# A denoising trunk on one core: one modulation vector moves from the first attention on TensorE into the first FFN on VectorE

## What is computed

```python
def adaln(cond, w, b):
    m = jax.nn.silu(cond) @ w + b                  # w_ada[li]: (1024, 9 * 1024)
    return [t[:, None, :] for t in jnp.split(m, N_MOD, axis=-1)]

def ffn_sublayer(x, shift, scale, gate, g_pre, g_post, w_in, w_out):
    h = modulate(rmsnorm(x, g_pre), shift, scale)  # x * (1 + scale) + shift
    a, b = jnp.split(h @ w_in, 2, axis=-1)
    h = (jax.nn.silu(a) * b) @ w_out
    return x + FFN_RES * gate * rmsnorm(h, g_post)

for li in range(DEPTH):
    mp = adaln(c_ctx[None, :], w_ada[li], b_ada[li])
    ms = adaln(c, w_ada[li], b_ada[li])
    yp = ffn_sublayer(yp, mp[0], mp[1], mp[2], ...)
    ...                                            # mixer with mp[3], mp[4], mp[5]
    yp = ffn_sublayer(yp, mp[6], mp[7], mp[8], ...)
```

## Time and profile before

| | |
|---|---|
| median of 3 runs | 3009.32 us (3008.97 to 3010.02) |
| the profiled execution | 3009.04 us, of it the span 3007.2 us |
| granted clock of TensorE, mean | 0.996 |
| busy: TensorE, VectorE, ScalarE, GpSimd | 2956.2, 2209.8, 1152.2, 561.6 us |
| sub-layer 0 (first FFN) | from about 36 to 314 us |
| sub-layer 1 (first attention) | from about 328 to 460 us |

### The profile page before, as it was taken

How to read it: one execution, slowest core, us unless ns; L and a number is a source line. 1 busy time by engine, 2 the same in 40 slices (tenths; PEclk the granted TensorE clock), 3 DMA queues, 4 the chain that set the end, 5 groups by cost and what they waited for, 6 DMA issues and landing times.

```text
span 3007.2 us, 46610 instructions
## 1 busy us (share of the span) xinstructions
PE 2956.2 (98%) x18194; PEld 2749.9 (91%) x18194; DVE 2209.8 (73%) x2897; ACT 1152.2 (38%) x1966; POOL 561.6 (19%) x586
## 2 busy tenths in 40 slices
PE   7999999999999999999999999999999999999999
PEld 6999889999999998999899999979999999889998
DVE  6888678887987657888888576768888888775444
ACT  4222664223322424222422365553224222664222
POOL 1111112112111112111211144631112111211001
PEclk9999999999999999999999999999999999999999
DMA  9667445665665445766566443337675766333443
GB/s 306 211 215 215 140 91 187 212 211 170 217 213 175 119 128 173 223 213 199 178 213 201 134 118 104 95 99 231 211 216 181 220 212 197 112 81 114 127 128 95
DMA packets 589696, 517.76 MB, mean 172 GB/s; under 512 B 66773, under 2 KB 523046, under 8 KB 587686
## 3 DMA queue, kind: packets, MB, share of 16 engines
q1 hardware_dynamic: 588918, 514.53, 56.6%
q10 hardware_dynamic: 560, 0.25, 0.0%
HBM read 510.37 MB, written 4.33 MB: 171 GB/s over the span
## 4 chain that ended last, share of the span: by engine, by line
PE 91%; issue 4%; DVE 2%; POOL 1%; ACT 1%; DMA 1%; SPq 0%; DVEq 0%; POOLq 0%; another core or an unknown queue 0%; ACTq 0%
PE bank L1698 19%; PE bank L1700 19%; PE bank L1699 19%; PE bank L1752 9%; PE bank L1751 9%; PE bank L1750 9%; PE bank L1725 1%; PE bank L619 1%; PE bank L1715 1%; PE bank L644 1%; DVE h_hi L2266 1%; DMA ada_first<-w_ada 1%; DVE h_lo L2276 0%; POOL hg_kr L1497 0%; PE bank L1783 0%
## 5 line engine op out<-in xcount | busy, mean ns | idle before, releaser
L1698 PE MATMUL bank<-h_hi,w_hi 128*128 128x384 f32 x3328 | 1120.6, 337 | 0.0
L1700 PE MATMUL bank<-h_hi,w_lo 128*128 128x384 f32 x3328 | 1114.6, 335 | 0.0
L1699 PE MATMUL bank<-h_lo,w_hi 128*128 128x384 f32 x3328 | 1113.8, 335 | 0.0
L1947 ACT ACTIVATE w_hi<-raw 128x1024 fp32r<-128x1024 f32 x646 | 681.1, 1064 | 1020.1 <-PE bank L1700 481.6
L2109 DVE TENSOR_TENSOR w_lo<-raw,w_hi 128x1024 fp32r<-128x1024 f32 x648 | 810.4, 1274 | 310.9 <-ACT w_hi L1947 305.7
L1698 PEld LDWEIGHTS bank<-h_hi,w_hi 128*128 128x128 f32 x3328 | 625.3, 188 | 10.9 <-ACT tmp L1966 1.6
L1699 PEld LDWEIGHTS bank<-h_lo,w_hi 128*128 128x128 f32 x3328 | 625.4, 188 | 6.1
L1700 PEld LDWEIGHTS bank<-h_hi,w_lo 128*128 128x128 f32 x3328 | 625.2, 188 | 0.0
L2136 DVE SCALAR_TENSOR_TENSOR fold<-ada_raw,cond,fold 128x1024 f32<-128x1024 f32 x462 | 616.4, 1390 | 0.1
L2455 POOL TENSOR_TENSOR h_lo<-tmp,h_hi 128x384 fp32r<-128x384 f32 x176 | 250.2, 1421 | 1762.9 <-DVE h_hi L2180 1762.9
L1752 PE MATMUL bank<-w_hi,h_lo 128*128 128x512 f32 x1056 | 414.0, 392 | 0.0
(11 more groups left out here) (204 smaller groups left out, 2420.1 us busy)
## 6 DMA issues: line engine op xcount, KB each, us to landing
raw<-w_ffn_in SPq DMA_DIRECT2D x352, 512.0 KB, 5.0
ada_raw<-w_ada SPq DMA_DIRECT2D x264, 512.0 KB, 4.2
raw<-w_ffn_out SPq DMA_DIRECT2D x176, 512.0 KB, 4.8
raw<-w_hgrn_in SPq DMA_DIRECT2D x40, 512.0 KB, 4.0
g_rows<-g_dram SPq DMA_DIRECT2D x12, 1024.0 KB, 6.7
raw<-w_attn_qkv SPq DMA_DIRECT2D x24, 512.0 KB, 5.5
raw<-w_conv_in SPq DMA_DIRECT2D x24, 512.0 KB, 4.9
ada_first<-w_ada SPq DMA_DIRECT2D x16, 512.0 KB, 11.0
```

The source lines that it names most:

```text
L1698: mm(out, wh, h_hi[:, k, :], start=(k == 0), stop=False)
L1699: mm(out, wh, h_lo[:, k, :], start=False, stop=False)
L1700: last = mm(out, wl, h_hi[:, k, :], start=False, stop=(k == DC - 1))
L1947: A(w_hi[:, b % RING, :], raw[:, b % RAW, :], ACT.Copy).then_inc(w_hi_made, 1)
```

## The change

Sub-layer 0 folds six units, 2 to 7, and sub-layer 1 makes none. The six begin at steps 0, 4, 8, 11, 15 and 18: the units that have three steps fold three, three and two slabs in them. In sub-layer 0 alone, slabs are loaded two blocks later in the sequence, sums are written three blocks later (and spread one block after that), and a unit is added four steps behind its reduction instead of two. Two units are then left over for the attention: one is added where the one was before, the second behind `normalize(1)`. TensorE no longer waits for `mods_made` ahead of the first scores of either attention.

```diff
-    units_of = {0: (2, 7), 1: (7, 8), 2: (8, 13), 3: (13, 17), 4: (17, 17), 5: (17, 22), 6: (22, 26), 7: (26, 26),
+    units_of = {0: (2, 8), 1: (8, 8), 2: (8, 13), 3: (13, 17), 4: (17, 17), 5: (17, 22), 6: (22, 26), 7: (26, 26),
                 8: (26, 31), 9: (31, 36), 10: (36, 36), 11: (36, 36)}
     units_end = [units_of[s][1] for s in range(12)]
-    FOLD_F = 4
+    UNIT_STARTS = {5: (0, 4, 8, 12, 16, 20), 6: (0, 4, 8, 11, 15, 18, 21)}
+
+    def unit_starts(s):
+
+        u0, u1 = units_of[s]
+        return UNIT_STARTS[max(u1 - u0, 5)]
 
     def sums_of(s):
 
         u0, u1 = units_of[s]
-        return {FOLD_F * (u - u0 + 1): u for u in range(u0, u1)}
+        return {unit_starts(s)[u - u0 + 1]: u for u in range(u0, u1)}
 
     def mods_of(s):
 
-        return {f + 2: u for f, u in sums_of(s).items()}
+        return {f + (4 if s == 0 else 2): u for f, u in sums_of(s).items()}
...
     def spreads_of(s):
 
-        return {at_a(f) + 11: u for f, u in sums_of(s).items()}
+        return {at_a(f) + (14 if s == 0 else 11): u for f, u in sums_of(s).items()}
 
     def slabs_at(s, f):
 
-        u0, u1 = units_of[s]
-        u = u0 + f // FOLD_F
-        return [(u, 2 * (f % FOLD_F) + n) for n in range(2)] if u < u1 else []
+        starts = unit_starts(s)
+        for i, u in enumerate(range(*units_of[s])):
+            length = starts[i + 1] - starts[i]
+            if starts[i] <= f < starts[i + 1]:
+                per = -(-DC // length)
+                first = per * (f - starts[i])
+                return [(u, k) for k in range(first, min(first + per, DC))]
+        return []
...
-        pe.wait_ge(mods_made, units_end[s])
+        if units:
+            pe.wait_ge(mods_made, units_end[s])
         scores(0)
...
         split(b0 + 9)
-        add_left_over()
+        add_left_over(0)
...
             normalize(2 * j + 1)
+            if j == 0:
+                add_left_over(1)
...
-                        slabs.setdefault(at_a(f) + 3 + n, []).append(slab)
+                        slabs.setdefault(at_a(f) + (5 if s == 0 else 3) + n, []).append(slab)
```

More of the change, by code:

```diff
@@ L2197, in mixer @@
                 elif ph.kind == "qkv":
-                    dve_attn(dve, s, split, ada_add, mod_add, lambda: [mod_fold(u) for u in left_over(s)])
+                    dve_attn(dve, s, split, ada_add, mod_add, lambda i: [mod_fold(u) for u in left_over(s)[i:i + 1]])
                 if ph.kind in ("hgrn", "qkv"):
```

## The result

The changed kernel takes 3018.61 us (median of 6 runs, 3017.65 to 3019.63), the kernel before in the same comparison 3009.47 (6 runs). The ratio is 1.0032, with a 95% interval from 1.0020 to 1.0045: slower by 9 us, where 4.0 were forecast and the range ended at +7.5. Taken again later on another occasion it was 1.0033 (1.0021 to 1.0044). So the sign was right and the size was not; the time lies outside the range.

What follows compares the result with a forecast made beforehand. TensorE, which never rests in the first FFN, was taken as the bound. Terms: 6.1 + 0.3 - 1.4 - 1.05 = +4.0 us on a median of 3009.32, giving 3013.3 us; range 3007.5 to 3016.8.

Steps and rivals of the forecast that it cites:

- The end of the FFN: Last steps of the first FFN: extra folds and a weight block held by the gains write make TensorE 6.1 us late.
- block 64: First FFN's 64th weight block, issued right behind the gains write: claimed to land 16.3 us after that write.
- block 61: First FFN's 61st weight block: TensorE claimed to begin it 4.2 us late, waiting for VectorE's multiplication of step 20.
- Rival 1: End of first FFN: the gains write holds no close follower; 2.1 us lost there, -0.4 in all, 3008.9; chance 0.20.
- seem to stand in line: Gains write in the first FFN: 2,048 single elements, with later blocks of SP's queue held until the write ends.
- The first attention: Removing unit 7's work there frees 4.27 us of TensorE; a late weight block leaves only 1.4 gained.
- A10: First attention's weight block behind the spread of unit 7: issued 1.7 us after unit 6's addition, landing 3.7 later.
- the boundary's 0.3: Between first FFN and attention: VectorE 0.65 us late at most, half of it idle time later, so 0.3 lost.
- from there a microsecond is a microsecond: First attention: each microsecond that A10 comes later was taken to cost just one microsecond.
- The second attention: TensorE's wait for the left-over unit before the first scores goes: 1.05 us gained.
- "Nothing" in the middle: Middle of the first FFN: unit 7's added folds and reductions are hidden behind TensorE and cost nothing.
- rival 2: First attention: A10 lands 7 us after issue, so 1.9 lost, not 1.4 gained; +7.3 us, 3016.6; chance 0.20.

Runs made afterwards that it cites:

- e13: On e4's kernel, the first FFN's gains transposed by TensorE and written as 16 rows of 128 numbers: 3009.01 us, ratio 0.9994.
- e9: On e4's kernel, the first FFN's gains written as 128 rows of 16 numbers, unpermuted and so wrong: 3007.76 us, ratio 0.9991.
- e3: The changed kernel with the first FFN's gains written three blocks sooner: 3016.29 us, ratio 1.0027.
- e12: The changed kernel again, nothing changed, with a second trace: 3020.04 us, ratio 1.0033.
- e2: The changed kernel with the two slabs of step 0 loaded behind blocks 3 and 4, as before: 3017.09 us, ratio 1.0031.
- e4: The changed kernel with the spread of unit 7's sums moved behind the loads of A10 and the block after it: 3009.15 us, ratio 1.0001.
- e5: The changed kernel with 14 unread matmuls on TensorE ahead of head 4's rotation in the first attention: 3017.19 us, ratio 1.0022.
- e6: On e4's kernel, the first FFN's gains written from ScalarE's DMA queue instead of SP's: 3014.65 us, ratio 1.0013.
- e1: The kernel before, unchanged, run and traced again: 3008.42 us, ratio 0.9999.
- e7: On e4's kernel, the six units begin at steps 0, 3, 6, 10, 14 and 17: 3009.86 us, ratio 1.0000.
- e11: The changed kernel with e7's unit starts and the gains written right behind block 63's load, ahead of waiting slabs: 3010.22 us, ratio 1.0000.

## Why the prediction was wrong

**The end of the FFN: right in its size, and in each term but one wait.** In the trace of after step 18 is 4.19 us late; with that added, the prediction said the write at 281.4 (281.48 measured), block 64 landed at 297.7 (297.5), TensorE late by 4.2 before block 61 (4.31), low parts ready at 310.6 (309.45 + 1.02 = 310.47). The tail is 6.14 to 6.46 us late in four traces (0.35 more by TensorE), 6.1 was forecast. The division held too: without the elements 2.1 was forecast, and 2.29 (e13) and 2.26 (e9) were measured; without the extra folds as well, 0.11 is left. What the forecast had wrong is what TensorE does between: of its two waits the second, some 2 us before the last chunk, came in e3, e9 and e13 (1.66 to 1.68) but not in after, e12, e2, e4, e5 and e6. In these six TensorE stands 3.7 to 4.9 us before block 61, and the clock falls to 0.5 for 3 to 7 us. In after this cost nothing, since the low parts came no sooner; that the size came out all the same is in part luck. Where the wait was longest (e5 and e6, 4.9 and 4.8) the tail is at +7.40 and +6.99. Rival 1 is out: the write holds a block 0.8 us behind it for 15.3 us.

The mechanism behind it was half right. I wrote that the blocks behind the write "seem to stand in line", and quoted the ring order. From another queue the write held the block just as long (15.7 us), so it is not the place in line. Nor are the elements themselves slow: 1,836 of them pass in a microsecond, and the packets of the loads behind take 2.3 us each instead of 0.15.

**The first attention: the load right, its price wrong.** A10 was issued 1.9 us after unit 6 was added (1.7 forecast) and landed in 3.9 (3.7). From the tail to the second heads the four traces gain 0.8 to 2.2 us (2.25, 2.15, 0.78 and 1.53; 1.1 was forecast, 1.4 less the boundary's 0.3). But a step of the prediction then failed: "from there a microsecond is a microsecond". TensorE's 3 us without work are followed by some 7 us at the granted clock of 0.5, and 1.96 to 2.59 us more are lost by the third heads, in all four traces with that rest and in none of the thirteen without it. So from the tail to the third heads these traces do not gain the 1.1 us of the forecast but lose 0.1 to 1.2: after and e12 0.1 to 0.3, e2 and e3 1.1 to 1.2. The latter two have one more stretch at 0.5, near 326 us, as before's trace has near 320 and e1's has not. This is the largest mis-sized term that the runs could name. The longest rests in the rows ahead of the prediction were 1.05 and 1.32 us, and I looked at none of 3 us, though before's trace has one of 2.87 with the low clock behind it, at 1966 us: I bounded how late the load could be and not what a rest brings behind it.

**The second attention: right.** 1.13 to 1.15 against 1.05.

**"Nothing" in the middle: right.** TensorE comes to step 18 on time, VectorE 0.35 us late. The start is not the change's: e1 has the slow one as well.

**What stays open.** Put together, the steps give 6.3 - 1.7 + 2.3 - 1.1 = 5.8 us (the means of the four traces); those traces, set to step 18, end at +5.92 to +7.87; the medians of their three kernels say 8.4 to 10.3. A part of this gap is the trace that all are measured against: set against e1's, the same kernel, the four end at +8.8 to +10.7. Between 2.6 and 4.5 us of the medians have no place. In e4 there is no such gap (its steps give +0.5, its median is 1.3 over before's), but in e6, without the late load, there is (+0.2 and 5.4). The clock is large enough for it. On e12's chip its six runs have a mean granted clock of 0.9940, the 28 of before 0.9958; 0.0018 of 3010 us is 5.5 us, an estimate from above, since a low clock costs nothing where TensorE waits. The short stretches at 0.5 recur at like places, near 1893 and 1975 us in all four traces (their own clock) and near 1944 and 1967 in before's, and I could not tie them to anything that the change does. Two smaller things are open as well: e6 against e4, and a stop of TensorE, ScalarE and VectorE of 1.1 to 1.4 us late in the second attention that four of the traces have (after, e12, e7, e11) and before's have not.

The range was wrong in its width for the same reason: its upper end came from rival 2, and no case had the clock in it, although before's stretches, cut finely enough, show it at 0.57 from 32 to 36 us and at 0.50 from 320 to 322 and from 1968 to 1970.

## What to carry to other kernels

A wait that appears on a full TensorE can be charged twice: for itself, and for the slow clock behind it, here 3 us and then 2.0 to 2.6. It is charged once where another engine holds the next step anyway, as at the end of this FFN, and here the waits of 1.3 us, and one of 2.81 in e3, had no slow clock behind them. So a small load must not be queued behind a step that waits for another engine if a weight block follows it, and if work is taken out of TensorE's stream, look at what wait it had covered. A DMA of many single elements is to be costed by how late it makes the loads behind it, here a landing 15.3 to 15.7 us after the issue instead of some 5, at both places and from both queues tried; a transposition ahead of it made that vanish.

## What the runs showed of the hardware

- 2,048 single 4-byte elements written to HBM: the next 512 KB block lands 16.1 us after the write when it is issued 0.8 us behind it, 17.3 when 2.0 behind, 18.5 when 2.8 behind on another queue. As 16 rows of 512 bytes: 5.3. The elements pass in about a microsecond; the 4 KB packets of the loads behind take 2.3 us each, against 0.15 before (e6).
- TensorE's granted clock fell to 0.5 at or behind each wait of 3.7 to 4.9 us before block 61 (six traces), behind each of 3.0 to 3.2 in the first attention (four), and behind 2.87 in before's third mixer; in e5, with idle work in place of most of the rest, it stayed at 1.00.
- The Trainium skill ("DMA: Bandwidth & Descriptors", Queues, rings and completion order) says that a DMA engine takes turns between the queues that have work for it, packet by packet. The trace of e6 agrees in that 43 packets of SP's queue came among the 1,836 elements of ScalarE's in one microsecond; but a block on the other queue does not get through early by it (15.7 us), since it is behind the elements that its packets are slow.
- At the start the same program runs at the lower clock for 4 us in some executions and for 14 in others, which moves its step 18 by up to 3.7 us (before and e1).
